# A transformer block's mixer: an input projection's parts taken in halves two pieces apart, its last groups put into the draining steps, and stick-breaking's mask added by products

## The chip, the cores and the metric

One core of a Trainium2 chip runs the whole program: TensorE (PE, its weight loads PEld), VectorE (DVE), ScalarE (ACT), GpSimd (POOL) and the DMA queues, of which only SyncE's (SP) is used here. The metric is the device time of one execution in microseconds. A change below about 0.5% can't be told from none: the three runs shown lie 0.41% apart.

## What is computed

Two blocks of a transformer on 512 tokens of width 1024. The change is in the second block, which has two layers, and in each layer in its `token_mixer_2`. Of the reference:

```python
proj = h @ w_in                       # 1024 -> 3072
qa, ka, va, qb, kb, vb, qc, kc, vc = jnp.split(proj, idx, axis=-1)
o_a = dilated_attention(...qa, ka, va)         # 6 heads, softmax, three dilated windows
o_b = differential_attention(...qb, kb, vb)    # 4 heads, two softmaxes per head
o_c = stick_breaking_attention(...qc, kc, vc)  # 6 heads
mixed = jnp.concatenate([o_a, o_b, o_c]) @ w_out

def stick_breaking_attention(q, k, v):         # per block of 128 queries
    valid = kpos[None, :] < (start + jnp.arange(Q_BLOCK))[:, None]
    z = jnp.einsum('bhqd,bhkd->bhqk', a, k)
    log_fail = jnp.where(valid, jax.nn.log_sigmoid(-z), 0.0)
    after = lax.cumsum(log_fail, axis=3, reverse=True) - log_fail
    wts = jnp.where(valid, jnp.exp(jax.nn.log_sigmoid(z) + after), 0.0)
    return jnp.einsum('bhqk,bhkd->bhqd', wts, v)
```

All of it is float32.

## The kernel before

Each layer is feed-forward, mixer, feed-forward. The mixer is two stages, one behind the other without a fence.

**The joint stage** (`w_pe`, `w_act`, `w_dve`) makes the input projection and, between its products, the dilated and the differential attention. A float32 product is made of three products in the reduced type fp32r: each operand is split into a high part (a copy by ACT, L3968) and a low part (a subtraction by DVE, L3971). In the profile's rows operands named `..._r` are such parts. The projection's weights are 18 units; `split_unit(l, u)` makes the parts of unit u on the engine that calls it. The products are 28 groups `gs` of 24 products each: 16 groups give one 128-column piece of queries or keys (`qk`, 512 moving columns), 12 give values (`vt`, 384 or 256 columns). The last four groups, 24 to 27, are the values of stick-breaking, all from unit 17, whose parts are 128x3072.

Attention runs in 20 steps k = 0 to 19 of two heads and one tile t of 128 queries: twelve "dil" steps, then eight "dif" steps, t going 0, 1, 2, 3 over and over, with keys up to the tile. PE's loop goes from k = -1 to 21: in iteration k it makes the scores of step k+1, turns (transposes) the weights of step k-1 and multiplies the values of step k-2, and in four gaps c = 0 to 3 it fills in products of the groups, `fill(k, c)`. DVE adds the biases and finds the maxima, ACT makes exponentials and copies. A planner written into the kernel deals the products of groups 4 to 27 out over the gaps: `share(k, r)` is what step k gets, r is found by bisection so that the sum comes out, and a product of 512 columns counts as 0.2326 us. `must` names the groups that have to be done by a step; the rest follows in order. In iterations 20 and 21 (the draining steps) nothing is filled in.

`beside(l, k, c)` is what ACT and DVE do beside `fill(k, c)`: ACT copies out the groups that end there, and both make the parts of a unit at the piece in which a certain earlier group begins (`split_at`). So DVE's low part stands at the same piece as ACT's high part, on which it waits. Both engines work through their instructions in the order written:

```python
for k in range(-1, N + 1):          # w_dve
    beside(l, k - 1, 3)
    unit(2 * k + 2)                 # biased, finish of an earlier head, highest, inverse
    beside(l, k, 0)
    beside(l, k, 1)
    unit(2 * k + 3)
    beside(l, k, 2)
```

**The stick-breaking stage** (`st_pe`, `st_act`, `st_dve`) goes over six heads i. PE makes scores z(i) (L4255), ACT takes softplus (L4263), DVE masks the four diagonal blocks of 128x128 by a multiplication (L4354, two instructions) and adds up rows for the sums (L4368 to L4371), PE adds the sums to z in PSUM (`after_sums`, L4277 and L4282), DVE clamps at 0 (L4385), ACT takes exp (L4331), DVE masks the four blocks again, PE multiplies by the values (L4295). PE's order is after_sums(i), values(i-1), z(i+2); z(i+2) needs the banks of head i, so it waits for clamped(i). For i = 0 PE makes two products for the differential heads' norm (`sub_sums`, L4311) in place of values; DVE does `sub_var` (L4377) behind them, ahead of clamped(0). z(0) and softplus(0) stand in iteration 20 of the joint stage. Then follows the output projection (L4412 to L4414).

Of the kernel before, what the change touches and what calls it, by code (L numbers as in the profile page):

```python
# [40 lines left out]
NEG = -1.0e30  # L41

def constants():
# [48 lines left out]
    sb = np.stack([sufneg, -np.ones((P, P), np.float32), (s < q).astype(np.float32)], 1)  # L94
# [41 lines left out]
def build(nc, a, out, known, final, upto, debug):  # L136
# [3 lines left out]
    with ctx:  # L140
# [70 lines left out]
        def program(l_):  # L211
# [2802 lines left out]
            def part_five():  # L3014
# [7 lines left out]
                ones2 = rest.take(P)  # L3022
                sbk = rest.take(3, P)
                lamp = rest.take(2, 4, 32)
# [24 lines left out]
                def lam_exp(l):  # L3049
                    if l is act:  # L3050
                        l.wait_ge(*past("lam_sums"))
                        l.did(S.activation(lam[:, 0:4], lam[:, 0:4], ACT.Exp).then_inc(l.sem, 1), "lam_exp")
# [716 lines left out]
                def mixer(l_, early, behind):  # L3769
# [79 lines left out]
                    split_at = {}  # L3849
                    for u, (_, before_) in enumerate(homes):  # L3850
                        if u > 3:
                            split_at.setdefault(first_of[max(u - 2, 0 if before_ is None else before_ + 1)], []).append(u)
# [66 lines left out]
                    def share(k, r):  # L3919
                        size = lambda j: (1 if j < DIL else 2) * width(steps[j][2]) if 0 <= j < N else 0  # L3920
                        inner = 0.5 + 0.0011 * (size(k + 1) + size(k - 1) + size(k - 2)) / 2
                        return max(0.8, r * (0.9 + 0.0042 * size(k + 1)) - inner) / 0.2326
                    total = sum(len(g["mms"]) * g["cost"] for g in gs[OPEN:])
                    lo_r, hi_r = 0.1, 20.0
                    for _ in range(50):
                        mid_r = (lo_r + hi_r) / 2
                        lo_r, hi_r = (mid_r, hi_r) if sum(share(k, mid_r) for k in range(-1, N)) < total else (lo_r, mid_r)
                    chunks, at_g, at_m, due = {}, OPEN, 0, 0.0
                    for k in range(-1, N + 2):
                        for c in range(4):  # L3930
                            here = chunks[k, c] = []
                            if k < N:
                                due += share(k, hi_r) / 4
                            while at_g < len(gs):
                                forced = c == 3 and (at_g <= must.get(k + 1, -1) or k >= N - 1)
# [15 lines left out]
                    for k in range(-1, N):  # L3951
# [10 lines left out]
                    def split_unit(l, u):  # L3962
                        x_, lo, hi, n = units[u]
                        if l is act:
# [3 lines left out]
                            l.did(S.activation(hi, x_, ACT.Copy).then_inc(l.sem, 1), nm, "hi", u)  # L3968
                        else:
                            l.wait_ge(*past(nm, "hi", u))  # L3970
# [7 lines left out]
                    def beside(l, k, c):  # L3978
# [6 lines left out]
                        for i in begun_in(k, c):  # L3985
                            for u in split_at.get(i, ()):
                                split_unit(l, u)

                    def w_pe(l):
# [104 lines left out]
                    def w_act(l):  # L4094
# [25 lines left out]
                        def out_(k):  # L4120
# [11 lines left out]
                        for u in split_at.get(3, ()):  # L4132
                            split_unit(l, u)
                        group_out(l, 3)
                        for k in range(-1, N + 2):
# [12 lines left out]
                            if k == N:  # L4148
                                softplus(l, 0)
                            out_(k - 2)  # L4150

                    def w_dve(l):
# [52 lines left out]
                        for u in split_at.get(3, ()):  # L4205
                            split_unit(l, u)
# [10 lines left out]
                    sp = region(extra, 2, 1280)  # L4217
                    wt = region(hT_at + 1536, 2, 1280)
# [22 lines left out]
                    def z(l, i):  # L4241
# [10 lines left out]
                        for s_ in (0, 1, 3, 2):  # L4252
# [3 lines left out]
                                            qk[rows_of(i), 10 + i // 2, s_ * P:T], start=(s_ != 3), stop=True, skip_group_check=(s_ == 3))  # L4256
                        l.did(ins.then_inc(l.sem, 1), nb, "z", i)
# [9 lines left out]
                    def st_pe(l):  # L4267
                        def after_sums(i):

                            l.wait_ge(*past(nb, "sp", i))  # L4270
# [28 lines left out]
                        for i in range(6):  # L4299
# [49 lines left out]
                    def st_dve(l):  # L4349
                        def mask(buf):  # L4350

                            for v in (buf[:, 0:1024].rearrange("p (a n) -> p a n", a=2)[:, :, 0:P],
                                      buf[:, 896:1152].rearrange("p (a n) -> p a n", a=2)):
                                l.did(V.tensor_tensor(v, v, sbk[:, 2, :].unsqueeze(1).to_broadcast([P, 2, P]), ALU.mult).then_inc(l.sem, 1))  # L4354
                        for i in range(7):
# [23 lines left out]
                            if i >= 1:  # L4379
# [158 lines left out]
```

## Time and profile before

| | |
|---|---|
| runs | 3374.6, 3372.78, 3360.88 us, median 3372.78 |
| profiled execution | 3374.64 us; span from first to last instruction 3372.9 us |
| busy over the span | PE 3172.8 (94%), DVE 1879.4 (56%), ACT 1260.7 (37%), POOL 179.9 (5%) |
| mean granted clock of PE | 0.978 of full speed |
| mixer of layer 0 | joint stage from 1698 us, stick-breaking from 1892 us, output projection alone from 1958 us |
| mixer of layer 1 | the same from 2717, 2911 and 2972 us |

Times in the rows are microseconds from the span's start. A row of the timeline has start, duration, engine, line, operation and what it writes and reads, and in brackets how long the engine had been idle and who released it. A matmul's duration is longer than the step from its start to the next one's start, since matmuls overlap; costs are read from starts. A float32 product that isn't split shows as two rows of instructions (x2).

### The profile page before, as it was taken

To read this page: it belongs to the slowest core of one execution; us is meant where nothing else is said; L and a number is where in the kernel's file an instruction comes from. 1 tells how busy PE (TensorE), PEld (TensorE's weight loads), DVE (VectorE), ACT (ScalarE), POOL (GpSimd) and SP (SyncE) were. 2 spreads that over 40 slices of the span, in tenths; PEclk is the share of its full clock that TensorE was granted. 3 is DMA by queue.
4 is the path that set the end of the run, shared out by engine and by line. 5 is a ranking of instruction groups with operands and counts; after the bars stand their busy time and mean duration, and the time that the engine had idled before them with its cause. 6 is when DMAs were issued, how large, how long until landed. Compare 5 with 4: busy or idle time off the path is not lost.

```text
span 3372.9 us, 60800 instructions
## 1 busy us (share of the span) xinstructions
PE 3172.8 (94%) x26392; PEld 2497.0 (74%) x26392; DVE 1879.4 (56%) x2783; ACT 1260.7 (37%) x2089; POOL 179.9 (5%) x168
## 2 busy tenths in 40 slices
PE   7999789999998889999999999999999999999999
PEld 6866677875443334999876679988999876679987
DVE  4457656557121114886355468854886354468853
ACT  3227433322000002453345544433443345554432
POOL 0003222221000000000000000000000000000000
PEclk9999789999999999999999999999999999999999
DMA  7140000114999996332321113323233321113322
GB/s 266 51 150 24 3 3 3 56 36 161 400 407 422 420 421 246 101 113 101 113 82 51 51 63 113 111 97 106 90 111 113 113 82 51 51 63 113 103 92 87
DMA packets 179763, 441.62 MB, mean 131 GB/s; under 512 B 7602, under 2 KB 107692, under 8 KB 154924
## 3 DMA queue, kind: packets, MB, share of 16 engines
q1 hardware_dynamic: 179500, 437.74, 35.2%
q8 instruction: 210, 3.44, 0.4%
q14 instruction: 53, 0.43, 0.0%
HBM read 435.62 MB, written 2.10 MB: 130 GB/s over the span
## 4 chain that ended last, share of the span: by engine, by line
PE 72%; DMA 8%; DVE 6%; ACT 4%; issue 3%; POOL 0%; SPq 0%; DVEq 0%; ACTq 0%; POOLq 0%
PE banks L3616 7%; PE banks L3619 7%; PE banks L3618 7%; PE banks L4008 6%; PE banks L2733 5%; PE banks L3737 4%; PE banks L3738 4%; PE banks L3736 4%; DMA ring<-in_exp_w_down 3%; DMA ring<-in_exp_w_gate 3%; DMA ring<-in_exp_w_up 1%; PE banks L349 1%; PE banks L393 1%; PE banks L1817 1%; PE banks L1445 1%
## 5 line engine op out<-in xcount | busy, mean ns | idle before, releaser
L2733 PE MATMUL banks<-ring,arena 128*64 128x512 f32 x1120 | 262.3, 604 | 36.7 <-DMA ring<-in_exp_w_gate 13.8
L3738 PE MATMUL banks<-tail_r,hid_r 128*128 128x512 f32 x704 | 279.7, 397 | 0.0
L3737 PE MATMUL banks<-ring_r,two_r 128*128 128x512 f32 x640 | 254.1, 397 | 0.0
L3736 PE MATMUL banks<-tail_r,two_r 128*128 128x512 f32 x640 | 250.7, 392 | 0.0
L2733 PEld LDWEIGHTS banks<-ring,arena 128*64 128x64 f32 x1120 | 86.2, 139 | 199.4 <-issue 185.0
L3616 PE MATMUL banks<-ring_r,tail_r 128*128 128x256 f32 x624 | 175.6, 281 | 9.0 <-DVE arena L3701 9.0
L304 DVE TENSOR_TENSOR hid_r<-arena,two_r 128x1024 fp32r<-128x1024 f32 x40 | 49.0, 1226 | 238.1 <-ACT two_r L301 223.8
L3618 PE MATMUL banks<-ring_r,tail_r 128*128 128x256 f32 x624 | 176.0, 282 | 0.0
L3616 PE MATMUL banks<-mix_r,tail_r 128*128 128x256 f32 x624 | 175.5, 281 | 0.0
L3618 PE MATMUL banks<-h_r,tail_r 128*128 128x256 f32 x624 | 174.7, 280 | 0.0
L3619 PE MATMUL banks<-mix_r,ring_r 128*128 128x256 f32 x608 | 171.1, 281 | 0.0
L3619 PE MATMUL banks<-ring_r 128*128 128x256 f32 x608 | 170.7, 281 | 0.0
L3738 PEld LDWEIGHTS banks<-tail_r,hid_r 128*128 128x128 f32 x704 | 132.2, 188 | 29.4
L301 ACT ACTIVATE two_r<-arena 128x1024 fp32r<-128x1024 f32 x40 | 42.4, 1060 | 284.6 <-PE banks L3738 258.1
L3491 ACT ACTIVATE tail_r<-ring 128x1024 fp32r<-128x1024 f32 x80 | 85.0, 1062 | 165.0 <-PE banks L3619 152.9
L3737 PEld LDWEIGHTS banks<-ring_r,two_r 128*128 128x128 f32 x640 | 120.1, 188 | 29.7
L3736 PEld LDWEIGHTS banks<-tail_r,two_r 128*128 128x128 f32 x640 | 120.7, 189 | 28.9
L304 DVE TENSOR_TENSOR ring_r<-ring,tail_r 128x2048 fp32r<-128x2048 f32 x48 | 110.0, 2293 | 29.0 <-ACT tail_r L301 29.0
L3616 PEld LDWEIGHTS banks<-ring_r,tail_r 128*128 128x128 f32 x624 | 117.7, 189 | 10.4 <-DVE arena L3701 10.4
L3616 PEld LDWEIGHTS banks<-mix_r,tail_r 128*128 128x128 f32 x624 | 117.6, 188 | 0.2
L3618 PEld LDWEIGHTS banks<-ring_r,tail_r 128*128 128x128 f32 x624 | 117.4, 188 | 0.0
L3618 PEld LDWEIGHTS banks<-h_r,tail_r 128*128 128x128 f32 x624 | 117.3, 188 | 0.2
(608 smaller groups left out, 8637.1 us busy)
## 6 DMA issues: line engine op xcount, KB each, us to landing
ring<-in_exp_w_gate SPq DMA_DIRECT2D x62, 1024.0 KB, 22.9
ring<-in_w_ffn_gate SPq DMA_DIRECT2D x44, 1024.0 KB, 5.3
ring<-in_w_ffn_up SPq DMA_DIRECT2D x44, 1024.0 KB, 5.4
ring<-in_exp_w_down SPq DMA_DIRECT2D x40, 1024.0 KB, 23.2
ring<-in_w_ffn_down SPq DMA_DIRECT2D x20, 2048.0 KB, 7.9
ring<-in_exp_w_up SPq DMA_DIRECT2D x38, 1024.0 KB, 18.8
ring<-in_w_in SPq DMA_DIRECT2D x13, 2048.0 KB, 10.0
arena<-in_exp_w_up SPq DMA_DIRECT2D x26, 1024.0 KB, 23.5
```

The costliest lines, as they stand in the source:

```text
L301: l.did(S.activation(hi, x_, ACT.Copy).then_inc(l.sem, 1), name, "hi", v)
L304: l.did(V.tensor_tensor(lo, x_, hi, ALU.subtract).then_inc(l.sem, 1), name, "lo", v)
L349: ins = TE.matmul(m[1](bank), m[2], m[3], start=m[4], stop=m[5])
L2733: ins = TE.matmul(banks[64 * e:64 * e + 64, b0 + hf, :], lhs(kk, e), w[:, k, hf * 512:(hf + 1) * 512], start=(kk == 0), stop=(kk == KD - 1))
L3491: l.did(S.activation(hi, x_, ACT.Copy).then_inc(l.sem, 1), sx, "hi", v, name)
L3616: TE.matmul(out_, a_hi[:, k0 + k, :], b_hi[:, k, :], start=(k == 0 and p not in FREE_BANK), stop=False, skip_group_check=True)
L3618: TE.matmul(out_, a_hi[:, k0 + k, :], b_lo[:, k, :], start=False, stop=False, skip_group_check=True)
L3619: ins = TE.matmul(out_, a_lo[:, k0 + k, :], b_hi[:, k, :], start=False, stop=(k == 3), skip_group_check=True)
L3736: TE.matmul(bank, h_hi, w_hi[:, c, ns], start=(f == 0), stop=False)
L3737: TE.matmul(bank, h_hi, w_lo[:, c, ns], start=False, stop=False)
L3738: ins = TE.matmul(bank, h_lo, w_hi[:, c, ns], start=False, stop=(f == NF - 1))
L4008: ins = TE.matmul(m[1](bank), m[2], m[3], start=m[4], stop=m[5])
```

## The change

1. **Parts.** `split_at` goes. Unit 4 is split with units 1 to 3 ahead of the loop. For units 5 to 17 a table gives the pieces: a unit of 128 columns is split whole, one of 256 in two halves of its eight k-slices, one of 384 (unit 17) in three parts. ACT's high part stands where it stood, counted in the new plan (further parts one piece later each); DVE's low part two pieces behind it, at most one piece ahead of the unit's first group.
2. **Plan.** Step -1 gets 4.0 us more. The last four groups are taken out of the plan of steps -1 to 18 and dealt evenly over the twelve gaps of iterations 19 to 21. Their copies out go with them.
3. **z(0) and softplus(0)** move from iteration 20 to iteration 19 (z(0) behind `fill(19, 1)`). z(1) waits for the last group in bank 5 only; the wait for the last group of all moves ahead of sub_sums.
4. **Mask.** The third constant of `k_sb` becomes 0 where valid and -1e9 where not. ACT makes an fp32r copy of it once (`barred_r`) and one of the identity in each mixer (`ident_r`). Behind the four products of z(i), PE adds `ident_r`-times-`barred_r` onto the four diagonal blocks. The four masking instructions a head (two behind softplus, two behind exp) go; after_sums waits for softplus itself and values for exp itself.

```diff
-    sb = np.stack([sufneg, -np.ones((P, P), np.float32), (s < q).astype(np.float32)], 1)
+    sb = np.stack([sufneg, -np.ones((P, P), np.float32), np.where(s < q, 0.0, OUT_OF).astype(np.float32)], 1)
...
                     if l is act:
+                        l.wait_ge(*smalls["second"])
+                        l.did(S.activation(barred_r, sbk[:, 2, :], ACT.Copy).then_inc(l.sem, 1), "barred")
...
-                        return max(0.8, r * (0.9 + 0.0042 * size(k + 1)) - inner) / 0.2326
-                    total = sum(len(g["mms"]) * g["cost"] for g in gs[OPEN:])
+                        return (max(0.8, r * (0.9 + 0.0042 * size(k + 1)) - inner) + (4.0 if k < 0 else 0.0)) / 0.2326
+                    LAST = len(gs) - NT
+                    units_in = lambda part: sum(len(g["mms"]) * g["cost"] for g in part)
+                    total, ending = units_in(gs[OPEN:LAST]), units_in(gs[LAST:])
...
-                            if k < N:
-                                due += share(k, hi_r) / 4
-                            while at_g < len(gs):
-                                forced = c == 3 and (at_g <= must.get(k + 1, -1) or k >= N - 1)
+                            due += share(k, hi_r) / 4 if k < N - 1 else ending / 12
+                            while at_g < (len(gs) if k >= N - 1 else LAST):
+                                forced = c == 3 and (at_g <= must.get(k + 1, -1) or k == N - 2 or k == N + 1)
...
+                    place = {i: 4 * (k + 1) + c for k, c in chunks for i in begun_in(k, c)}
+                    halves_of = {"act": {}, "dve": {}}
+                    for u in range(5, len(units)):
+                        free_at = max(u - 2, 0 if homes[u][1] is None else homes[u][1] + 1)
+                        cuts = {P: (0, 8), 256: (0, 4, 8), 384: (0, 3, 6, 8)}[unit_cols[u][1]]
+                        for n_, ks in enumerate(zip(cuts, cuts[1:])):
+                            end_ = place[first_of[u]] - 1
+                            at_lo = min(place[first_of[free_at]] + n_ + 2, end_)
+                            halves_of["act"].setdefault(min(at_lo, place[first_of[free_at]] + n_), []).append((u,) + ks)
+                            halves_of["dve"].setdefault(at_lo, []).append((u,) + ks)
...
-                        for i in begun_in(k, c):
-                            for u in split_at.get(i, ()):
-                                split_unit(l, u)
+                        for u, k0, k1 in halves_of[l.name].get(4 * (k + 1) + c, ()):
+                            split_unit(l, u, k0, k1)
...
-                            elif k == N:
-                                z(l, 0)
...
+                            if k == N - 1:
+                                z(l, 0)
                             fill(k, 2)
...
+                        l.did(S.activation(ident_r, ident, ACT.Copy).then_inc(l.sem, 1), nb, "ident")
...
-                            l.wait_ge(*past(nm, "read", len(gs) - 1))
+                            l.wait_ge(*past(nm, "read", max(i_ for i_ in bank_at if bank_at[i_] == 5)))
...
+                        for s_ in (0, 1, 3, 2):
+                            b, c, _ = where[s_]
+                            ins = TE.matmul(banks[:, 3 * (i % 2) + b, c:c + P], ident_r, barred_r, start=False, stop=True, skip_group_check=True)
...
-                            l.wait_ge(*past(nb, "sp", i))
+                            l.wait_ge(*past(nb, "ln", i))
...
-                            l.wait_ge(*past(nb, "w", h))
+                            l.wait_ge(*past(nb, "exp", h))
...
+                                l.wait_ge(*past(nm, "read", len(gs) - 1))
...
-                                mask(sp[:, i % 2, :])
-                                l.name_last(nb, "sp", i)
...
-                                l.wait_ge(*past(nb, "exp", h))
-                                mask(wt[:, h % 2, :])
-                                l.name_last(nb, "w", h)
```

## Rows read from the trace of the kernel before

**Rows 1.** Both mixers, stretches: length; busy by engine (instructions); PE's clock; DMA, GB/s.
```profile
1698.00:1958.00 260.00, 245.01 (x1314) 178.77 (x1315) 123.73 (x252) 129.87 (x242) 0.00 (x0) 0.96 0.14 48
2717.00:2977.00 260.00, 245.33 (x1338) 180.56 (x1339) 127.73 (x254) 135.30 (x247) 0.00 (x0) 0.98 0.15 52
```

**Rows 2.** PE's waits, layer 0's mixer: for whom; us in all, times, longest.
```profile
PE banks L4255 <- DVE arena L4385: 4.1, 2, 2.7
PE banks L4041 <- DVE ring L4164: 3.0, 1, 3.0
PE banks L4036 <- DVE ring L4164: 2.5, 2, 1.6
PE banks L4053 <- DVE ring L4185: 2.5, 1, 2.5
PE banks L4053 <- ACT arena L4117: 2.2, 4, 0.7
```

**Rows 3.** PE's waits in layer 1's mixer, where they differ.
```profile
PE banks L4041 <- DVE ring L4164: 3.4, 1, 3.4
...
PE banks L4053 <- ACT arena L4117: 1.2, 2, 0.7
```

**Rows 4.** Stretches around the waits, columns as in rows 1.
```profile
1715.00:1735.00 20.00, 18.40 (x86) 14.84 (x86) 8.78 (x25) 8.41 (x19) 0.00 (x0) 0.91 0.17 54
1835.00:1850.00 15.00, 8.92 (x48) 5.66 (x50) 6.69 (x10) 8.45 (x15) 0.00 (x0) 0.89 0.00 0
1930.00:1940.00 10.00, 8.57 (x27) 4.76 (x26) 7.06 (x13) 8.01 (x7) 0.00 (x0) 0.84 0.01 2
2850.00:2875.00 25.00, 19.13 (x92) 13.59 (x91) 14.36 (x27) 13.93 (x34) 0.00 (x0) 0.86 0.00 1
```

**Rows 5.** Timeline of DVE at the low parts of units 16 and 17.
```profile
1838.37 1.23 DVE L3971 TENSOR_TENSOR ring_r<-ring,ffn_r 128x1024 fp32r<-128x1024 f32 x1 [3.37 <-ACT ffn_r L3968]
...
1845.96 3.36 DVE L3971 TENSOR_TENSOR ring_r<-ring,ring_r 128x3072 fp32r<-128x3072 f32 x1 [4.91 <-ACT ring_r L3968]
```

**Rows 6.** Timeline of PE, iterations 19 and 20: the turns.
```profile
1884.60 0.44 PE L4053 MATMUL banks<-arena 128*128 128x128 f32 x2 [0.51 <-ACT arena L4117]
...
1889.99 0.66 PE L4053 MATMUL banks<-arena,ring 128*128 128x128 f32 x4 [0.69 <-ACT arena L4117]
```

**Rows 7.** Timeline of PE and PEld: fp32r products of 256 columns, one behind another.
```profile
1698.37 0.28 PE L4006 MATMUL banks<-h_r,ffn_r 128*128 128x256 f32 x1
1698.49 0.28 PE L4006 MATMUL banks<-mix_r,ring_r 128*128 128x256 f32 x1
...
1698.37 0.19 PEld L4006 LDWEIGHTS banks<-mix_r,ring_r 128*128 128x128 f32 x1
```

**Rows 8.** Timeline of PE: from float32 products (L4072) back to fp32r.
```profile
1833.48 0.50 PE L4008 MATMUL banks<-h_r,ffn_r 128*128 128x512 f32 x1
1833.81 0.39 PE L4008 MATMUL banks<-mix_r,ring_r 128*128 128x512 f32 x1
1834.05 0.39 PE L4008 MATMUL banks<-mix_r,ffn_r 128*128 128x512 f32 x1
```

**Rows 9.** Timeline of DVE and PE in the stick-breaking stage: z(2), z(3) and z(5).
```profile
1900.31 1.22 DVE L4377 TENSOR_SCALAR arena<-banks 128x1024 f32<-128x1024 f32 x1 [2.18 <-PE banks L4311]
1901.45 1.48 DVE L4385 TENSOR_SCALAR arena<-banks 128x1280 f32<-128x1280 f32 x1
...
1902.99 4.63 PE L4255 MATMUL banks<-arena 64*128 64x512 f32 x8 [2.71 <-DVE arena L4385]
...
1916.18 2.42 PE L4255 MATMUL banks<-arena 64*128 64x512 f32 x8
...
1931.20 0.76 DVE L4354 TENSOR_TENSOR arena<-arena 128x256 f32<-128x256 f32 x2 [4.10 <-ACT arena L4263]
...
1932.81 1.48 DVE L4385 TENSOR_SCALAR arena<-banks 128x1280 f32<-128x1280 f32 x1
...
1934.34 2.42 PE L4255 MATMUL banks<-arena 64*128 64x512 f32 x8 [1.43 <-DVE arena L4385]
```

More of the change, by code:

```diff
@@ L41 @@
 NEG = -1.0e30
+OUT_OF = -1.0e9
 def constants():
@@ L3022, in part_five @@
                 ones2 = rest.take(P)
+                rest.at += -rest.at % 8
+                sbk_at = rest.at
                 sbk = rest.take(3, P)
+                barred_r = parts_of("barred_r", sbk_at + 2 * P, P)(sbk_at + 2 * P, P)
                 lamp = rest.take(2, 4, 32)
@@ L3848, in mixer @@
                         first_of.setdefault(g["unit"], i)
[L3849 to L3852, printed above, removed]
                     yield nm, units[0], gs[0:2]
@@ L3926, in mixer @@
                         mid_r = (lo_r + hi_r) / 2
-                        lo_r, hi_r = (mid_r, hi_r) if sum(share(k, mid_r) for k in range(-1, N)) < total else (lo_r, mid_r)
+                        lo_r, hi_r = (mid_r, hi_r) if sum(share(k, mid_r) for k in range(-1, N - 1)) < total else (lo_r, mid_r)
                     chunks, at_g, at_m, due = {}, OPEN, 0, 0.0
@@ L3950, in mixer @@
                     bank_at, bank_free, last_in = {i: i for i in range(OPEN)}, {}, {i: i for i in range(OPEN)}
-                    for k in range(-1, N):
+                    for k in range(-1, N + 2):
                         for c in range(4):
@@ L3960, in mixer, with split_unit @@
                     bank_of = lambda i: bank_at[i]
-                    def split_unit(l, u):
+                    place = {i: 4 * (k + 1) + c for k, c in chunks for i in begun_in(k, c)}
[8 more added lines that the diff above has]
+                            halves_of["dve"].setdefault(at_lo, []).append((u,) + ks)
+                    def split_unit(l, u, k0=0, k1=KD):
                         x_, lo, hi, n = units[u]
+                        x_, lo, hi = (ap[:, k0:k1, :] for ap in (x_, lo, hi))
                         if l is act:
@@ L3967, in split_unit @@
                                 l.wait_ge(*past(nm, "used", homes[u][1]))
-                            l.did(S.activation(hi, x_, ACT.Copy).then_inc(l.sem, 1), nm, "hi", u)
+                            l.did(S.activation(hi, x_, ACT.Copy).then_inc(l.sem, 1), nm, "hi", u, k0)
                         else:
-                            l.wait_ge(*past(nm, "hi", u))
+                            l.wait_ge(*past(nm, "hi", u, k0))
                             l.did(V.tensor_tensor(lo, x_, hi, ALU.subtract).then_inc(l.sem, 1), nm, "lo", u)
@@ L4131, in w_act @@
                         split_unit(l, 3)
-                        for u in split_at.get(3, ()):
-                            split_unit(l, u)
+                        split_unit(l, 4)
                         group_out(l, 3)
@@ L4147, in w_act @@
                             beside(l, k, 2)
-                            if k == N:
+                            if k == N - 1:
                                 softplus(l, 0)
                             out_(k - 2)
+                        beside(l, N + 1, 3)
                     def w_dve(l):
@@ L4204, in w_dve @@
                         split_unit(l, 3)
-                        for u in split_at.get(3, ()):
-                            split_unit(l, u)
+                        split_unit(l, 4)
                         group_out(l, 2)
@@ L4217, in mixer @@
                     sp = region(extra, 2, 1280)
+                    ident_r = ffn_r(extra + 3328, P)
                     wt = region(hT_at + 1536, 2, 1280)
@@ L4256, in z @@
                                             qk[rows_of(i), 10 + i // 2, s_ * P:T], start=(s_ != 3), stop=True, skip_group_check=(s_ == 3))
+                        if i == 0:
+                            l.wait_ge(*past("barred"))
+                            l.wait_ge(*past(nb, "ident"))
+                        for s_ in (0, 1, 3, 2):
+                            b, c, _ = where[s_]
+                            ins = TE.matmul(banks[:, 3 * (i % 2) + b, c:c + P], ident_r, barred_r, start=False, stop=True, skip_group_check=True)
                         l.did(ins.then_inc(l.sem, 1), nb, "z", i)
@@ L4349, in st_dve @@
                     def st_dve(l):
[L4350 to L4354, printed above, removed]
                         for i in range(7):
```

## The prediction

> **What bounds the kernel now.** I read the stretches of both mixers first, since nothing outside them is edited but one small copy. PE is busy for 245.0 and 245.3 of 260 us, DVE and ACT for about half [rows 1]. The list of PE's waits says where the rest is [rows 2, 3]. In its words: z waits for the clamp (4.1 us a mixer, twice), dil scores wait for the bias addition (2.5, of which 1.6 is one wait), dif scores wait for it (3.0 and 3.4, one wait each), the turns wait for DVE's finished weights (2.5, one wait) and for ACT's copies (2.2 and 1.2). The granted clock is 0.96 and 0.98 on average over the two mixers, so the low level takes 0.04 x 260 + 0.02 x 260 = 15.6 us of them together [rows 1]. The stretches show that it follows the waits [rows 4].
>
> The waits' cause is on DVE's timeline. The low part of unit 16 stands at the same piece as ACT's high part, so DVE waits 3.37 us for ACT and then works 1.23; unit 17's costs 4.91 of waiting and 3.36 of work [rows 5]. Behind these stand, in DVE's order, the bias addition and the finish that PE's scores and turns wait for. DVE isn't too busy; it is held.
>
> **The change part by part.** I sum over both layers, against the profiled execution's 3374.64 us (3372.9 of span and 1.7 around it, which stays). That execution is 1.9 us above the median of the three runs.
>
> *The start.* In iteration -1 the planner gives 2.8 us of products before, and 6.3 after (worked through with its own 0.2326 us a product). PE's wait of 1.6 us behind them [rows 2] is for a bias addition that DVE makes behind the low part of unit 5. That part now stands two gaps later, behind that addition, and PE comes 3.5 us later: the wait goes, 2 x 1.6 = 3.2. The low clock around it, (1 - 0.91) x 20 = 1.8 in layer 0 [rows 4], I let go with it. The other 0.9 of the same line is a bias addition behind a low part too; two pieces of distance free it: 1.8. Sum 6.8 (bounds 3.2, if the clock stays and the 0.9 too, and 6.8).
>
> *The middle.* The waits of the turns and the dif scores without the 1.2 of iterations 19 and 20 (below) are 3.0 + 2.5 + 1.0 and 3.4 + 2.5 + 0 = 12.4 [rows 2, 3]. Low parts 13 to 16 now stand behind their high parts by two gaps, and unit 17 comes in thirds in iteration 18, the longest (9.1 us of products). I follow iteration 15, the thinnest of the dif steps (2.6 us of products, 3.5 before): ACT's order is two exponentials, a normalisation, the turn's copy, the high part of unit 15; PE's second turn comes about 1.2 us too early for the copy, and in iteration 16 again about 1.0. So I leave 2.4 a layer: 12.4 - 4.8 = 7.6 won. The low clock there is 0.11 x 15 + 0.14 x 25 = 5.2 [rows 4]; waits of half the size leave some of it, I take two thirds, 3.5. Sum 11.1 (bounds 0, if the waits only change place, and 17.6, if none is left).
>
> *The last groups.* 4 groups x 24 products x 0.757 x 0.2326 = 16.9 us a layer move to iterations 19 to 21. There PE waited for only 0.51 + 0.69 = 1.2 us [rows 6], so they don't fill idle time worth 16.9; they only leave the earlier steps shorter and these longer. What can be won is the 1.2, twice: 2.4. The cost is that fp32r products now stand between float32 ones more often. From float32 back to fp32r the first step is 0.33 us long where the next is 0.24 [rows 8], so 0.1; I take the same for the way there, 0.2 for a pair. Iterations 19 to 21 have four more such pairs: 2 x 4 x 0.2 = 1.6. Sum 0.8 (bounds -1.6 and 2.4). Steps 0 to 18 lose 16.9 + 3.5 - 0.9 = 19.5 us of products a layer; I count nothing for it, because DVE's and ACT's halves of idle time [rows 1] should cover 1.0 us a step. That is the cover to watch (rival C). z(0) and softplus(0) earlier bring nothing by themselves: what waits behind after_sums(0) is another thing.
>
> *Stick-breaking, what goes.* DVE's masks are 0.76 us each [rows 9], 12 a layer, and PE hardly waits for them: at z(5) only. There softplus(4) came late behind two ACT copies, and DVE did mask, sums, clamp in that order, all ahead of z(5), which waited 1.43 us [rows 9]. Without the mask the chain is 0.87 shorter (mask and its hand-over), and PE comes later by its own four added products: the wait goes, 2 x 1.43 = 2.9, and layer 0's low clock behind it, 0.16 x 10 = 1.6 [rows 4]. The larger wait, 2.71 us at z(2), stays: sub_var (1.22) and the clamp (1.48) follow sub_sums one after the other, and nothing of that is edited [rows 9]. So does the low clock behind it; z(2) took 4.63 where z(3) took 2.42 [rows 9].
>
> *Stick-breaking, what comes.* 4 products of 128 columns a head, 48 in all, on the engine that has no room: z, sums and values follow one another without a gap there. No row has an fp32r product of 128 columns. By columns it is half of the 0.12 between products of 256 [rows 7], 0.06; it can hardly be over 0.24, a tenth of z's 2.42 for 1,280 float32 columns [rows 9]. I take 0.09, halfway between 0.06 and the 0.12 of the wider product, since its weights are loaded anew each time. With a pair of switches a head: 12 x (0.2 + 4 x 0.09) = 6.7 (bounds 12 x 0.44 = 5.3 and 12 x 1.16 = 13.9). The Trainium skill (TensorE: Matmul & The Clock Gate, section Back-to-back issue gap) gives about 81 ns for a load-and-product pair of 128 columns; the estimate by that page would be 12 x (0.2 + 0.32) = 6.2, half a microsecond less. No run here shows that figure.
>
> The two copies are under 0.4 us each and hidden: at the mixer's start PE has 48 products of 0.12 us [rows 7], 5.8 us, ahead of the parts that the identity's copy delays; the other is made once, in the first feed-forward. The moved wait for group 27 is long over when sub_sums comes.
>
> Sum: 6.8 + 11.1 + 0.8 + 2.9 + 1.6 - 6.7 = 16.5, so 3374.64 - 16.5 = 3358.1.
>
> **The rivals.**
>
> *B: the added products cost their weight load too.* A load takes 0.19 [rows 7]; in a line with 0.06 of columns a product is 0.25, a head 0.2 + 1.0, 14.4 in all in place of 6.7: 3365.8. Four float32 passes give nearly the same (13.9). Against it: between the products of 256 columns loads of 0.19 start every 0.12, so they overlap [rows 7]. The Trainium skill (TensorE: Matmul & The Clock Gate, section The mechanism) says that a load overlaps running products only when their row groups differ, and here they are the same; by that rule B would hold, and this trace does not bear it out at 256 columns.
>
> *C: the steps get too thin, slower.* Each of the steps 0 to 18 loses about 1.0 us of the products that cover DVE's and ACT's chains. In the dif steps the chain (scores, bias, maximum, two exponentials, finish) is longest; iterations 11 to 18 lose 10.4 us a layer. If all of that comes back as PE's waits for DVE and ACT: 3358.1 + 20.8 = 3378.9; if all 39 us of steps 0 to 18, 3397. It decides from 16.5 of the 39 on. For it: PE's waits in turns were for such chains [rows 2]. Against: DVE is busy for 124 of 260 us [rows 1], and the long waits were behind held low parts [rows 5].
>
> *D: the middle is wholly freed.* No 4.8 left, the rest of the clock there (1.7) back, products at 0.06 (1.4): 3350.2. For it: 3.37 and 4.91 of DVE's waiting [rows 5] are all due to the place of the low parts. Against: the copy that I followed in iterations 15 and 16.
>
> *E: the middle doesn't move.* DVE waits for a high part at its new place just as long, since ACT's own order holds it: 3358.1 + 11.1 = 3369.2. Against: two pieces later ACT has come past its exponentials.
>
> **How the numbers follow.** A, the forecast with leftovers between 3353 and 3363: 0.45. D 0.25, B 0.12, C 0.10, E 0.08. Half a per cent of the median 3372.78 is 16.9, so faster means below 3355.9: D and a good third of A, 0.42. Slower means above 3389.6, the worse half of C: 0.05. The rest, 0.53, is within. The range for 8 in 10 takes in D with the 3 to 4 us by which clocks differ from run to run below it, B and E, and leaves out C: 3345 to 3371. A alone reaches from 3353 to 3363.
>
> **What would show it.** Right: PE's waits for the bias additions of lines 4036 and 4041's kind under 1 us a layer; the turns' waits about 2 us; z's wait for the clamp at 2.7 a layer instead of 4.1; z's eight rows followed by four products of under 0.5 us together, head after head at 8.9 us instead of 8.3; no long idle time of DVE in front of a low part. Wrong: a new line of waits in iterations 8 to 18 of over 5 us a layer (C), added products at 0.2 us or more (B), or low clock in places where PE no longer waits.

## The result, and the profile after

The changed kernel takes 3344.3 us (median of 9 runs, 3338.9 to 3350.7). The kernel before, run beside it, takes 3364.7 (median of 9, 3356.1 to 3374.6). The ratio is 0.9935, interval 0.9923 to 0.9947: 21.9 us faster, 17.8 to 25.9. I forecast 3358.1 with a range down to 3345, so the time lies 0.7 us below the range.

Below are two views of the changed kernel, answering to [rows 1] and [rows 2]: the stretches of 260 us of both mixers, and PE's waits in layer 0's mixer (layer 1 has the same five lines). Line 4051 is now that of the dil scores, 4056 of the dif scores, 4068 of the turns, 4180 of the bias addition, 4201 of the finish, 4271 of z, 4278 of the added products, 4401 of the clamp.

```profile
1691.50:1951.50 260.00, 253.34 (x1382) 185.73 (x1383) 122.60 (x235) 137.95 (x252) 0.00 (x0) 0.98 0.17 58
2700.00:2960.00 260.00, 253.58 (x1389) 186.35 (x1390) 122.46 (x234) 137.59 (x252) 0.00 (x0) 0.99 0.17 60
```

```profile
PE banks L4271 <- DVE arena L4401: 2.7, 1, 2.7
PE banks L4068 <- ACT arena L4132: 2.3, 4, 1.0
PE banks L4021 <- DVE h_r L3168: 1.6, 1, 1.6
PE banks L4023 <- ACT arena L399: 0.8, 1, 0.8
PE banks L4068 <- DVE ring L4201: 0.4, 1, 0.4
```

PE stands still for 6.4 to 6.7 us of 260 in place of 15. Every wait for a bias addition is gone, and so is the one at z(5). What is left is the wait at z(2), 3.5 us that the forecast put at 2.4 (turns and copies of groups), and in layer 0 the last 0.2 of the untouched 1.6, most of which lies ahead of the stretch.

The low parts of units 16 and 17 in DVE's timeline, answering to [rows 5]:

```profile
1834.62 1.22 DVE L3987 TENSOR_TENSOR ring_r<-ring,ffn_r 128x1024 fp32r<-128x1024 f32 x1
...
1844.99 2.62 DVE L3987 TENSOR_TENSOR ring_r<-ring,ring_r 128x1152 fp32r<-128x1152 f32 x2
...
1850.59 0.95 DVE L3987 TENSOR_TENSOR ring_r<-ring,ring_r 128x768 fp32r<-128x768 f32 x1
```

None of them has a wait in brackets; before, they had 3.37 and 4.91. Where the time went is best seen by stages: from the first product to z(1), and from z(1) to the end of the last values. First the kernel before, in the execution of the rows ahead of the prediction; the columns are those of [rows 1].

```profile
1698.17:1892.45 194.28, 183.60 (x1092) 141.88 (x1092) 91.72 (x195) 90.65 (x207) 0.00 (x0) 0.98 0.18 62
2717.66:2911.06 193.40, 183.53 (x1092) 142.17 (x1093) 91.71 (x195) 90.77 (x207) 0.00 (x0) 0.98 0.18 62
1892.45:1958.43 65.98, 61.84 (x227) 37.08 (x225) 32.37 (x56) 39.06 (x36) 0.00 (x0) 0.90 0.02 6
2911.06:2972.11 61.05, 56.91 (x227) 34.37 (x225) 32.36 (x56) 39.05 (x36) 0.00 (x0) 0.97 0.02 7
```

The same four stretches of the changed kernel:

```profile
1691.73:1876.73 185.00, 181.41 (x1096) 139.52 (x1097) 93.20 (x202) 92.32 (x211) 0.00 (x0) 1.00 0.16 56
2699.89:2884.90 185.01, 181.42 (x1097) 139.54 (x1097) 93.19 (x202) 92.31 (x211) 0.00 (x0) 1.00 0.16 56
1876.73:1941.80 65.07, 62.24 (x246) 38.40 (x245) 21.89 (x29) 37.69 (x34) 0.00 (x0) 0.92 0.09 33
2884.90:2948.59 63.69, 60.86 (x246) 37.75 (x245) 21.89 (x29) 37.69 (x34) 0.00 (x0) 0.95 0.09 33
```

The four sum to 514.7 us before and 498.8 after: 15.9 less, where I had forecast 16.5. All of it is in the joint stage (387.7 to 370.0), whose clock is now full throughout; the stick-breaking stage didn't get shorter (127.0 to 128.8 in these two executions). Outside the mixers, which nothing edits but one copy, the span fell by 8.1 as well (2858.2 to 2850.1). The last two runs below are about that.

### The profile page after: what moved, and what is told of

Its sections match the earlier page's. It is cut to its first block, busy times and chain, and to the rows that moved or that the text cites. A ratio compares the mean times of both kernels' runs of the same rounds, so it can differ in the third digit from the quotient of the medians.

```text
span 3348.8 us, 60877 instructions
## 1 busy us (share of the span) xinstructions
PE 3169.2 (95%) x26440; PEld 2493.3 (74%) x26440; DVE 1861.8 (56%) x2741; ACT 1261.1 (38%) x2098; POOL 179.6 (5%) x168
## 4 chain that ended last, share of the span: by engine, by line
PE 74%; DMA 8%; DVE 6%; ACT 3%; issue 2%; POOL 0%; SPq 0%; DVEq 0%; POOLq 0%; ACTq 0%
PE banks L3624 7%; PE banks L3622 7%; PE banks L3625 7%; PE banks L4023 7%; PE banks L2734 5%; PE banks L3744 4%; PE banks L3742 4%; PE banks L3743 4%; DMA ring<-in_exp_w_down 3%; DMA ring<-in_exp_w_gate 3%; DMA ring<-in_exp_w_up 1%; PE banks L350 1%; PE banks L394 1%; PE banks L1818 1%; PE banks L1673 1%
## 5 line engine op out<-in xcount | busy, mean ns | idle before, releaser
L2734 PE MATMUL banks<-ring,arena 128*64 128x512 f32 x1120 | 262.5, 605 | 36.8 <-DMA ring<-in_exp_w_gate 13.8
## 6 DMA issues: line engine op xcount, KB each, us to landing
ring<-in_w_in SPq DMA_DIRECT2D x13, 2048.0 KB, 10.1
```

Source lines behind the costliest of these rows:

```text
L2734: ins = TE.matmul(banks[64 * e:64 * e + 64, b0 + hf, :], lhs(kk, e), w[:, k, hf * 512:(hf + 1) * 512], start=(kk == 0), stop=(kk == KD - 1))
```

## The experiments

All compare with the kernel before, run on the same chip; the chips differ between e, f and g, so between these groups ratios are compared and not medians. "Mixers" is the sum of the four stretches above in the run's own profile; "outside" is the rest of the span.

| kernel | median us | ratio (interval) | mixers | outside |
|---|---|---|---|---|
| before, two profiles | | | 514.7, 515.4 | 2858.2, 2846.4 |
| changed, two profiles | 3344.3 | 0.9935 (0.9923 to 0.9947) | 498.8, 497.4 | 2850.1, 2851.8 |
| e1: parts alone | 3346.2 | 0.9947 (0.9933 to 0.9962) | 496.6 | 2842.6 |
| e2: plan alone | 3371.6 | 1.0017 (1.0006 to 1.0028) | 522.2 | 2847.9 |
| e3: mask alone | 3362.2 | 0.9996 (0.9987 to 1.0006) | 516.4 | 2846.9 |
| e4: changed, without the mask | 3346.8 | 0.9945 (0.9929 to 0.9961) | 499.6 | 2849.2 |
| f1: changed, first clamp ahead | 3330.1 | 0.9905 (0.9891 to 0.9919) | 485.3 | 2839.5 |
| f2: changed, products doubled | 3347.6 | 0.9958 (0.9945 to 0.9971) | 502.4 | 2843.3 |
| f3: parts and mask | 3336.4 | 0.9923 (0.9911 to 0.9936) | 494.8 | 2840.4 |
| f4: changed, no distance | 3359.7 | 0.9988 (0.9978 to 0.9999) | 516.6 | 2843.4 |
| g1: parts, mask, clamp ahead | 3327.2 | 0.9890 (0.9873 to 0.9906) | 482.6 | 2842.4 |
| g2: parts, clamp ahead | 3331.0 | 0.9896 (0.9881 to 0.9911) | 479.3 | 2848.8 |

**e1: the parts alone** (edit 1 of the change, in the kernel before).

```diff
...
-                        for i in begun_in(k, c):
-                            for u in split_at.get(i, ()):
-                                split_unit(l, u)
+                        for u, k0, k1 in halves_of[l.name].get(4 * (k + 1) + c, ()):
+                            split_unit(l, u, k0, k1)
...
```

> The parts alone (halves and thirds, low parts two pieces behind), with the old plan, z(0) in its old place and DVE's masks. Theory P (PE waits behind low parts that hold DVE, so the parts are the gain): the start's 3.2, the 1.8 of the other late bias addition and 11 of the middle go, 3350 where before is 3366, 14 to 18 us less than before; PE's waits of dif scores and dil scores for bias additions are gone, the turns' waits for ACT stay at 2 to 3 a layer. Rival G (the groups taken out of the steps are the gain): under 6 us less. Rival M (the mask is): under 6 us less.

17.8 us faster by the ratio, and 18.5 less in the mixers (against 515.1, the mean of before's two profiles). PE's waits of layer 0's mixer:

```profile
PE banks L4260 <- DVE arena L4390: 4.1, 2, 2.7
PE banks L4060 <- ACT arena L4124: 2.6, 4, 1.0
PE banks L4013 <- DVE h_r L3162: 1.6, 1, 1.6
```

No bias addition is waited for, not even at the start, although the start has no more products than before. The parts alone do the whole of what I gave to "start" and "middle": the joint stage falls by 21.1 for both layers, while the stick-breaking stage, which this edit doesn't touch, was 2.6 longer in this profile.

**e2: the plan alone** (edits 2 and 3).

```diff
...
-                            if k < N:
-                                due += share(k, hi_r) / 4
+                            due += share(k, hi_r) / 4 if k < N - 1 else ending / 12
...
```

> The plan alone: 4.0 us more in step -1, the last four groups in the draining steps, z(0) and softplus(0) an iteration earlier; parts whole and at one piece on ACT and DVE as before, masks on DVE. Theory P: only the start's wait (3.2, with its clock up to 5) and the 2.4 of the draining steps are won, 1.6 is lost to more changes between float32 and fp32r; unit 17's low part (3.4 us) still holds DVE in a step that has become thinner, so the middle's waits stay or grow: 0 to 6 us less than before. Rival G: 12 us less or more.

A miss: 5.7 us slower (2.0 to 9.4 by the interval), 7.1 more in the mixers, of which 4.6 in the joint stage. PE's waits in layer 0's mixer:

```profile
PE banks L4054 <- ACT arena L4118: 4.6, 4, 1.9
PE banks L4054 <- DVE ring L4187: 4.2, 3, 3.0
PE banks L4257 <- DVE arena L4388: 4.1, 2, 2.7
PE banks L4037 <- DVE ring L4166: 2.0, 3, 1.4
```

And DVE's timeline, at two low parts, in the same kernel:

```profile
1805.53 1.23 DVE L3972 TENSOR_TENSOR ring_r<-ring,ffn_r 128x1024 fp32r<-128x1024 f32 x1 [5.19 <-ACT ffn_r L3969]
...
1834.70 1.23 DVE L3972 TENSOR_TENSOR ring_r<-ring,ffn_r 128x1024 fp32r<-128x1024 f32 x1 [4.63 <-ACT ffn_r L3969]
```

This is rival C's mechanism at work: with fewer products in a step, PE reaches the turns earlier and stands there for a DVE that is still held. The waits at turns are 8.8 us here against 4.7 before [rows 2], those for bias additions 2.0 against 5.5. In the changed kernel DVE isn't held, and C costs little.

**e3 and e4: the mask** alone in the kernel before, and the changed kernel without it (masks on DVE as before).

Of e4's edit (e3 adds these lines):

```diff
...
-                        for s_ in (0, 1, 3, 2):
-                            b, c, _ = where[s_]
-                            ins = TE.matmul(banks[:, 3 * (i % 2) + b, c:c + P], ident_r, barred_r, start=False, stop=True, skip_group_check=True)
...
```

> The mask alone: four products a head in place of DVE's four masks, all else as before. Theory P: the added products cost 12 x 0.45 = 5.4 us (by the changed kernel's trace; 6.7 by the prediction), the wait at z(5) gives 2.9 back and its clock up to 1.6: between 1 us faster and 3 us slower than before. Rival M: 8 us faster or more, since DVE's masks lay on the chain of every head.

> The changed kernel with DVE's masks put back and the added products taken away: parts and plan together. Theory P: within 3 us of the changed kernel (5.4 of products saved, 2.9 and up to 1.6 of the wait at z(5) and its clock back), so 18 to 22 us less than before. Rival M: 8 us or more above the changed kernel.

The mask alone can't be told from no change, and in the mixers it is 1.3 longer. With the rest of the change it is 1.5 shorter. In both pairs the wait at z(5) goes: z's waits for the clamp are 8.3 us in the kernels with DVE's masks and 5.4 with products, both layers together. In layer 0's mixer, e3 (products) and then e4 (DVE's masks):

```profile
PE banks L4263 <- DVE arena L4392: 2.7, 1, 2.7
```

```profile
PE banks L4268 <- DVE arena L4399: 4.1, 2, 2.7
```

**f1: the first clamp ahead of sub_var**, in the changed kernel. My theory of the stick-breaking stage was that the low clock there [rows 4] follows the 2.71 us wait at z(2), which comes only from the order of two instructions on DVE, so that both would go together. The rival was a clock that stays low there whatever PE does.

```diff
-                            if i == 1:
-                                l.wait_ge(*past(nb, "sub_sums"))
-                                l.did(V.tensor_scalar(sq2, banks[:, 6:8, :], 1.0 / HD, NORM_EPS, ALU.mult, ALU.add).then_inc(l.sem, 1),
-                                      nb, "sub_var")
...
                                 l.did(V.tensor_scalar(wt[:, h % 2, :], flat(h), 0.0, None, ALU.min).then_inc(l.sem, 1), nb, "clamped", h)
+                                if i == 1:
+                                    l.wait_ge(*past(nb, "sub_sums"))
+                                    l.did(V.tensor_scalar(sq2, banks[:, 6:8, :], 1.0 / HD, NORM_EPS, ALU.mult, ALU.add).then_inc(l.sem, 1),
+                                          nb, "sub_var")
```

> The changed kernel with clamped(0) ahead of sub_var on DVE, so that z(2) waits for the clamp alone, which runs beside sub_sums. Theory W (the low clock at z(2) to after_sums(1) is due to the 2.71 us wait ahead of it): the wait goes, 2 x 2.71 = 5.4, and z(2) takes 2.4 us in place of 4.6 and 3.2, which with the slow products behind it gives up to 8 more: 7 to 13 us below the changed kernel. Rival V (the low clock there comes with z's kind of products, not with the wait): 4 to 6 us below, z(2) still slow.

First the changed kernel at this place: DVE's two instructions, z(2) behind them, and the stretch that follows.

```profile
1885.04 1.23 DVE L4393 TENSOR_SCALAR arena<-banks 128x1024 f32<-128x1024 f32 x1 [3.16 <-PE banks L4334]
1886.18 1.48 DVE L4401 TENSOR_SCALAR arena<-banks 128x1280 f32<-128x1280 f32 x1
1887.71 4.63 PE L4271 MATMUL banks<-arena 64*128 64x512 f32 x8 [2.71 <-DVE arena L4401]
```

```profile
1890.00:1900.00 10.00, 10.00 (x31) 6.26 (x30) 1.83 (x4) 6.18 (x6) 0.00 (x0) 0.63 0.00 0
```

The same place with the clamp ahead:

```profile
1872.77 1.49 DVE L4397 TENSOR_SCALAR arena<-banks 128x1280 f32<-128x1280 f32 x1 [1.44 <-PE banks L4304]
1874.49 1.22 DVE L4400 TENSOR_SCALAR arena<-banks 128x1024 f32<-128x1024 f32 x1 [0.23 <-PE banks L4334]
...
1874.39 2.42 PE L4271 MATMUL banks<-arena 64*128 64x512 f32 x8
```

```profile
1875.00:1885.00 10.00, 10.00 (x45) 6.15 (x44) 3.00 (x5) 9.36 (x9) 0.00 (x0) 1.00 0.00 1
```

z(2) takes 2.42 in place of 4.63, and the clock is full. The stick-breaking stage is 57.63 long in either layer; in the changed kernel's two profiles it was 64.0 on average. By the ratios it is 10.1 faster than the changed kernel, by the mixers 12.8. What the same wait costs in clock is not always the same: from z(2) to z(3) it is 8.33 us at full clock with DVE's masks (g2), and 13.20, 9.97, 11.65 and 11.65 in the four mixers of the kernel before.

**f2: the added products made twice.** It measures what one costs. The second set adds -1e9 once more where a key is out of the window already.

```diff
-                        for s_ in (0, 1, 3, 2):
+                        for s_ in (0, 1, 3, 2, 0, 1, 3, 2):
```

> The changed kernel with the four mask products of each head made twice (masked scores get -2e9 in place of -1e9; the output is the same): 48 more products and no more changes between float32 and fp32r. By the step from z to the sums in the changed kernel's trace, 0.50 us a head, of which about 0.2 was taken for the changes: 0.075 a product, 48 x 0.075 = 3.6 us more. If the prediction's rival B held (0.25 each, load in line): 12 us more. By columns alone (0.06): 2.9 more.

Changed kernel, the four products and what follows them:

```profile
1903.50 0.66 PE L4278 MATMUL banks<-barred_r,ffn_r 128*128 128x128 f32 x4
1904.00 1.07 PE L4299 MATMUL banks<-arena 128*128 128x512 f32 x2
```

Doubled:

```profile
1896.78 1.11 PE L4278 MATMUL banks<-barred_r,ffn_r 128*128 128x128 f32 x8
1897.73 1.07 PE L4299 MATMUL banks<-arena 128*128 128x512 f32 x2
...
1896.78 0.97 PEld L4278 LDWEIGHTS banks<-barred_r,ffn_r 128*128 128x128 f32 x8 [0.33 <-issue]
```

From start to start it is 0.50 us for four and 0.95 for eight: 0.45 / 4 = 0.113 a product, and 0.05 for the way in and out. So the products are nearer to my upper neighbour (0.12 of a 256-column product [rows 7]) than to half of it, and the pair of switches is far under the 0.2 that I took. The steps from z(3) to z(4) say it more closely: 8.33 us before, 8.77 with four (1901.15 to 1909.92) and 9.22 with eight. So the first four cost 0.45 as the second four do, and hardly anything is left for the switches. Over the 12 heads that is 5.4, where I had expected 3.6; the mixers of f2's one profile are 4.3 longer. The Trainium skill (TensorE: Matmul & The Clock Gate, section Back-to-back issue gap) gives about 81 ns for a load-and-product pair of 128 columns; this trace has 113 ns for pairs in fp32r, and the measurement decides. Rival B's 0.25 is out.

**f3: parts and mask with the old plan** (e1's and e3's edits together).

> Parts and mask with the old plan (no groups moved to the draining steps, no 4.0, z(0) and softplus(0) in their old place). Theory P (the plan brings nothing once the parts don't hold DVE): within 2 us of the changed kernel, on either side. Rival G2 (the plan pays only together with parts and mask): 5 us or more above the changed kernel.

The ratio is 0.9923 where the changed kernel's is 0.9935, which is 4.0 us; the intervals overlap, so the times alone don't settle it. The mixers say the same: 494.8 against 498.8 and 497.4. The joint stage is 183.7 a layer in place of 185.0. So by the profiles the plan costs 2.7 in the joint stage of both layers, and e4 less e1 has 3.0 there. Neither of the two expectations was right: the plan doesn't bring nothing, it costs.

**f4: the changed kernel without the distance**, DVE's low part at ACT's piece again; halves and thirds, plan and mask stay.

```diff
-                            at_lo = min(place[first_of[free_at]] + n_ + 2, end_)
+                            at_lo = min(place[first_of[free_at]] + n_, end_)
```

> The changed kernel with the low parts at the same piece as the high parts again (distance 0 in place of 2), unit 17 still in thirds and the new plan kept. Theory P (the distance frees DVE): DVE waits again for high parts, 2 to 3 us at each unit, and PE's waits for bias additions and turns come back in part: 4 to 12 us above the changed kernel. Rival S (it's the cutting of unit 17 that matters): within 2 us of the changed kernel.

More than I expected came back: 17.8 by the ratios, 18.5 in the mixers, 15.9 of it in the joint stage. DVE at the low part of unit 16 and PE's largest waits for turns and scores in layer 0's mixer:

```profile
1829.31 1.23 DVE L3987 TENSOR_TENSOR ring_r<-ring,ffn_r 128x1024 fp32r<-128x1024 f32 x1 [4.63 <-ACT ffn_r L3984]
```

```profile
PE banks L4068 <- ACT arena L4132: 4.5, 4, 1.9
...
PE banks L4068 <- DVE ring L4201: 2.1, 3, 1.0
...
PE banks L4051 <- DVE ring L4180: 1.3, 3, 0.7
```

Without the distance the mixers are as long as those of the kernel before (516.6 and 515.1): with all else in place, the two pieces hold the whole gain. Rival E is out: in the changed kernel the low parts don't wait, and here they do. No run has the distance without the halves and thirds, so what the cutting adds to it isn't shown.

**g1 and g2: the best of these put together**, old plan, parts, clamp ahead; g1 with the mask by products, g2 with DVE's masks.

> The kernel before with the parts (1), the mask by products (4) and the first clamp placed ahead of sub_var, and with the old plan. Theory W (low clock behind the 2.71 us wait; the plan costs): what the reordered clamp brought to the changed kernel, 14 us in runs, of which 2 x 2.7 is the wait and the rest is the clock behind it, comes on top of the parts with the mask (3336.4): 3322 to 3330, and 0 waits of z for the clamp. Rival (the gains are the same gain counted twice): within 4 us of parts with mask, 3332 to 3340.

> As the run with parts, mask and reordered clamp, but with the mask by multiplications on DVE as before (no added products). If the mask by products pays only because it takes DVE's masks out of the chain ahead of z's waits for the clamp, then with the clamp reordered it costs its products: this kernel is 0 to 6 us faster than the one with them. If the runs' 8 to 10 us for the mask (parts with mask against parts alone) are a gain of its own, this kernel is 5 to 10 us slower.

g1 has the lowest median, 37 us (32 to 43) under the kernel before, though its interval overlaps those of f1 and g2. f3's gain and f1's are not the same gain counted twice. The two stages of its layer 0:

```profile
1684.04:1867.73 183.69, 181.01 (x1097) 140.12 (x1097) 91.70 (x198) 90.69 (x210) 0.00 (x0) 1.00 0.19 67
1867.73:1925.33 57.60, 57.48 (x247) 35.85 (x245) 23.52 (x32) 38.94 (x36) 0.00 (x0) 1.00 0.01 4
```

What the mask is worth is not settled by the times. g2's mixers are 3.3 us shorter than g1's; its median is 3.8 longer, and the intervals overlap almost wholly. In the profiles the products cost what they add (5.4) less the wait at z(5), and that is a small loss once the clamp is ahead. By the ratios, though, the kernel with products is the faster one in all four pairs (e3 and before 1.3 us, changed and e4 3.4, f3 and e1 8.1, g1 and g2 2.0), in none clear of the intervals. No run explains that.

**Both kernels once more**, for a second profile.

> The kernel before once more, for a second profile. If the base of my sum was off by the one execution that it was made against: the mixers again at 513 to 517 us together, and the time outside them at 2840 to 2851 instead of 2858.2, so a time of 3356 to 3367. If the first profile was typical: outside within 3 us of 2858.

> The changed kernel once more, for a second profile. By my sum the mixers are again 14 to 18 us shorter than those of the kernel before (497 to 501 us together); outside them it is 2840 to 2851 as in the kernel before. If something outside the mixers was really made faster, its time outside is over 5 us below that of the kernel before in the same call.

The kernel before took 3363.6 us this time, 11.1 less than in the execution that I read. Its mixers are 515.4 long, the same within 0.7; outside it is 2846.4 in place of 2858.2. From the first mixer to the second it is 759.2 and 759.4 us, behind the second 400.8 and 400.7, so all of the 11.8 lies ahead of the first mixer, which began at 1698.17 and at 1686.32. A stretch there, in the first profile and in the second:

```profile
400.00:600.00 200.00, 178.17 (x4890) 152.26 (x4884) 122.10 (x235) 79.66 (x198) 46.80 (x54) 0.91 0.01 3
```

```profile
400.00:600.00 200.00, 179.25 (x5236) 156.41 (x5236) 123.02 (x238) 82.91 (x207) 47.97 (x57) 0.98 0.01 4
```

It is the first block, with the same code and a granted clock of 0.91 in one execution and 0.98 in the other. By these two figures the lost clock differs by 0.07 x 200 = 14 us, about the size of the 11.8. In this stretch 0.91 is the lowest of all 14 profiles; the others have 0.92 to 0.98. Over all 14 profiles of this study the first mixer begins between 1679.9 and 1698.2, and the profile that I read is the latest of them, by 5.8.

The changed kernel's second profile (3351.1 us) has mixers of 497.4 and 2851.8 outside: not shorter than the kernel before outside the mixers.

## Why the prediction was right or wrong

**The step that failed is the base.** The terms are summed "against the profiled execution's 3374.64 us", and the range allowed "the 3 to 4 us by which clocks differ from run to run". That execution lies 9.9 above the median of nine runs of the same kernel (3364.7), it is the slowest of all 56 runs of that kernel in this study (3354.1 to 3374.6), and its excess is in the first block. The same sum from 3364.7 gives 3348.2, and the measured 3344.3 is 3.9 below that; so of the 13.8 us by which the forecast missed, 9.9 are the base and 3.9 the sum. One warning stood in what I had: the three runs shown lie 13.7 apart, with 3360.9 among them, where the range allowed 3 to 4. Their median, 3372.8, would hardly have been a better base: it is 8.1 too high as well. That 0.91 is a low clock for the first block couldn't be told from the one profile that I had.

**The sum came out near, in part by luck.** Mean mixers of two profiles each: 515.1 before and 498.1 after, 17.0 less, against 16.5. By the runs the gain is 21.9 (17.8 to 25.9), and 16.5 lies below that. The mechanism is the forecast one: low parts that hold DVE at the place of the high parts (e1, f4). But several term sizes were off: the gain of the parts was put 3.2 too small and the plan 3.5 to 3.8 too good. That they cancel is luck. By stages, both layers together (joint stage before 387.2, stick-breaking 127.9, means of two profiles):

| step of the prediction | forecast | measured | from |
|---|---|---|---|
| start and middle (the parts) | -17.9 | -21.1 | e1: joint 183.15 + 183.00 |
| last groups and more at the start (the plan) | -0.8 | +2.7 to +3.0 | joint: changed less f3, e4 less e1 |
| wait at z(5) | -2.9 | -2.9 | 8.3 less 5.4 |
| added products | +6.7 | +5.4 | 12 heads of 8.77 less 8.33 |
| clock behind z(5) | -1.6 | -1.4 to -4.7 | the rest of the stick-breaking stage, below |

- *What PE stands still for.* Of the 15 us in a stretch of 260 I gave 1.6 to the wait ahead of the first product. The stretches begin 0.2 and 0.7 before that product, so nearly all of the 15 are the other waits. No term of the sum hangs on it.
- *Start.* The waits for the bias addition behind unit 5's low part went. My reason gave the credit to both the later low part and the added products; e1 shows that the low part alone does it.
- *Middle.* Left are 3.5 us of PE's waits a layer outside z(2) and the start in place of 2.4; one turn's copy by ACT is 1.0 late, as I had followed. But the clock came back wholly, not by two thirds: 1.00 over the joint stage where it was 0.97 to 0.98.
- *Last groups.* The sign was wrong. They fill no idle time, as I wrote, but the plan (edits 2 and 3) costs 1.3 to 1.5 a layer. 0.9 of it is waits of PE (3.5 a layer in place of e1's 2.6). The other 0.4 to 0.5 is a longer busy time of PE for the same products (181.4 in place of f3's 181.0). That would fit the added switches between float32 and fp32r, but no run shows that it is they, nor which of the plan's edits costs what.
- *Products.* 0.11 each in place of 0.09, the switches at most 0.05 in place of 0.2.
- *Stick-breaking.* 127.9 before, 128.1 after (two profiles each). Five sixths of 5.4 come in here, 4.5 (z(0)'s stand in the joint stage), and 2.9 of wait go, so about 1.4 of clock went too. From e1 to f3 (130.5 to 127.4) the same reckoning gives 4.7. Since the stage varied from 61.1 to 66.0 between layers of the kernel before, this is weak.
- *z(2).* It kept its 2.71 wait in every mixer, and the low clock behind it, as forecast.

**The rivals.** A's mechanism is what the traces show; its range was not reached, because of the base. B and E are out (f2, f4). C's mechanism is real (e2) but weak once DVE is free. D's time is nearest to the runs, and of its reasons the clock came true; but waits were left in the middle, and no product costs 0.06.

**What stays open.** By the runs the change wins 20 to 22 us, by the profiles' mixers 17.0. The difference is the size of the differences between executions outside the mixers, and no run here places it. For f3 and f1 it goes the same way (25.9 against 20.3, 32.0 against 29.8), for e1 and g2 slightly the other way (17.8 against 18.5, 35.0 against 35.8).

## What to carry to other kernels

An instruction that waits for another engine at the place where that engine is only just told to work holds everything behind it in its own order: put it later, as far as its user allows, before moving or thinning any work. Two pieces were enough here, and no other distance was run. Where a wait of a few microseconds on TensorE is found, look at the clock behind it as well, since exchanging two instructions of the other engine may win twice the wait. Make a sum against the median of many runs, let the range be as wide as the runs lie apart, and read the clock of the stages that nothing edits in more than one profile: here they moved a single execution by more than half of the change.

## What the runs showed of the hardware that I had not expected

- A wait of 2.71 us at z(2) is followed by a clock of 0.63 over 1890 to 1900 us with PE busy throughout; taking the wait away (f1) gave back 7.4 us of clock for 5.4 of waiting, both layers together.
- An fp32r product of 128 columns takes 0.113 us, hardly less than one of 256 (0.12 [rows 7]), with a new weight load each. By columns it would be half of that 0.12, 0.06, so something else sets the pace; f2's eight loads take 0.97 together and start every 0.11, so it may be they, but no run shows it. The Trainium skill (TensorE: Matmul & The Clock Gate, section The mechanism) says that a load overlaps running products only when their row groups differ, and in another sentence there also when it goes to the background weight buffer. Here the row groups are the same, and at 256 columns loads of 0.19 still fit between products that start every 0.12 [rows 7], so the first rule alone is not borne out. At 128 columns the steps leave 0.05 beyond the columns, and the trace doesn't decide it.
- The same program's first block ran at 0.91 and at 0.98 of full clock over the same 200 us in two executions, and one came 11.8 us later to the first mixer than the other.
